# Attention probabilities turned by VectorE squares and a trip through DRAM instead of on TensorE

## The reference

```python
aq, ak, av, bq, bk, bv, cq, ck, cv, cg, gates = jnp.split(h @ w_in[l], split_points, axis=-1)
y_a = diff_attention(qa, ka, va, lam, lam_init, a_subln[l])   # 4 heads: softmax - lam * softmax, width 128
y_b = chunk_attention(qb, kb, vb, b_rel_bias[l])              # 8 heads: softmax with relative bias, width 64
y_c = retention(qc, kc, vc, cg.astype(f32), c_out_norm[l])    # 4 heads: scores * decay, no softmax
```

## Time and profile before

| | |
|---|---|
| median of 3 runs | 1818.6 us (1818.33 to 1820.05) |
| profiled execution, first to last instruction (span) | 1816.7 us |
| time of that execution outside the span | not recorded apart; median less span is 1.9 us |
| PE busy | 1797.5 us, 99% |
| POOL busy | 1365.0 us, 75% |
| DVE busy | 942.8 us, 52% |
| ACT busy | 905.1 us, 50% |
| DMA | 366.61 MB, mean 202 GB/s |
| granted TensorE clock, mean | 0.999 of full speed |

### The profile page before, as it was taken

One profiled execution on the slowest core, in us unless ns is written; L12 is line 12 of the kernel. 1 busy time (PEld: TensorE's weight loads), 2 busy tenths in 40 slices (PEclk: granted clock), 3 DMA queues, 4 the chain that ended last, 5 costly groups with the idle time before them and its releaser, 6 DMA issues.

```text
span 1816.7 us, 25068 instructions
## 1 busy us (share of the span) xinstructions
PE 1797.5 (99%) x9322; PEld 1482.3 (82%) x9322; DVE 942.8 (52%) x1756; ACT 905.1 (50%) x1337; POOL 1365.0 (75%) x568
## 2 busy tenths in 40 slices
PE   6999999999999999999999999999999999999999
PEld 5888888887889888887888888888888878888887
DVE  4673766678655524776553230714095865143152
ACT  3334424764456644455554644464445565545442
POOL 2624544559868898987689798969897858888885
PEclk9999999999999999999999999999999999999999
DMA  9853885748775775565466566567655645656653
GB/s 366 299 201 93 278 301 164 196 157 301 245 279 188 221 216 194 172 209 165 132 187 195 175 195 195 193 184 232 195 195 181 186 139 163 194 160 211 190 194 128
DMA packets 200697, 366.61 MB, mean 202 GB/s; under 512 B 32868, under 2 KB 54356, under 8 KB 200020
## 3 DMA queue, kind: packets, MB, share of 16 engines
q1 hardware_dynamic: 197568, 357.39, 61.6%
q10 hardware_dynamic: 3028, 7.86, 1.1%
HBM read 364.12 MB, written 6.13 MB: 204 GB/s over the span
## 4 chain that ended last, share of the span: by engine, by line
PE 98%; DMA 0%; ACTq 0%; ACT 0%; DVE 0%; POOL 0%; issue 0%; DVEq 0%
PE ps L1258 26%; PE ps L1260 26%; PE ps L1259 26%; PE ps L1384 3%; PE ps L1385 3%; PE ps L1386 3%; PE ps L1949 1%; PE ps L1951 1%; PE ps L1950 1%; PE ps L1306 1%; PE ps L1876 1%; PE ps L1655 1%; PE ps L1626 1%; PE ps L1636 1%; PE ps L1516 1%; PE ps L1921 1%
## 5 line engine op out<-in xcount | busy, mean ns | idle before, releaser
L616 POOL TENSOR_TENSOR w_lo<-raw,w_hi 128x1024 fp32r<-128x1024 f32 x556 | 1346.0, 2458 | 403.4 <-ACT w_hi L654 382.2
L1258 PE MATMUL ps<-w_hi,act_rows_r 128*128 128x512 f32 x2064 | 814.8, 395 | 3.2 <-POOL w_lo L616 3.1
L1260 PE MATMUL ps<-w_hi,act_rows_r 128*128 128x512 f32 x2064 | 804.8, 390 | 0.0
L1259 PE MATMUL ps<-w_lo,act_rows_r 128*128 128x512 f32 x2064 | 804.5, 390 | 0.0
L654 ACT ACTIVATE w_hi<-raw 128x1024 fp32r<-128x1024 f32 x556 | 571.1, 1058 | 359.4 <-DMA raw<-in_ffn_w_up 96.5
L1258 PEld LDWEIGHTS ps<-w_hi,act_rows_r 128*128 128x128 f32 x2064 | 387.9, 188 | 89.9 <-issue 8.6
L1260 PEld LDWEIGHTS ps<-w_hi,act_rows_r 128*128 128x128 f32 x2064 | 387.8, 188 | 81.8
L1259 PEld LDWEIGHTS ps<-w_lo,act_rows_r 128*128 128x128 f32 x2064 | 388.1, 188 | 77.2
L2604 DVE STREAM_TRANSPOSE ps<-proj 32x256 f32<-32x256 f32 (+1 forms) x384 | 166.6, 434 | 6.5
L2585 DVE TENSOR_TENSOR proj<-proj,ps 128x1024 f32<-128x1024 f32 (+1 forms) x18 | 20.4, 1132 | 252.2 <-PE ps L1260 247.8
L1384 PE MATMUL ps<-act_rows_r,w_hi 128*128 128x512 f32 (+1 forms) x288 | 101.4, 352 | 0.0
(11 more groups left out here) (245 smaller groups left out, 1559.9 us busy)
## 6 DMA issues: line engine op xcount, KB each, us to landing
raw<-in_w_in SPq DMA_DIRECT2D x120, 512.0 KB, 3.8
raw<-in_ffn_w_gate SPq DMA_DIRECT2D x88, 512.0 KB, 4.3
raw<-in_ffn_w_up SPq DMA_DIRECT2D x88, 512.0 KB, 4.3
raw<-in_ffn_w_down SPq DMA_DIRECT2D x88, 512.0 KB, 3.4
proj<-in_ada_w SPq DMA_DIRECT2D x39, 512.0 KB, 7.8
pt<-in_ada_w SPq DMA_DIRECT2D x38, 512.0 KB, 6.4
raw<-in_pool_w_in SPq DMA_DIRECT2D x32, 512.0 KB, 7.4
raw<-in_na_w_in SPq DMA_DIRECT2D x32, 512.0 KB, 5.4
```

The lines of the kernel that those rows point to most:

```text
L616: pool.tensor_tensor(w_lo[:, s, :], raw[:, s, :], w_hi[:, s, :].bitcast(F32), ALU.subtract).then_inc(lo_done, 1)
L1258: pe.matmul(o, h, hi, start=start, stop=False)
L1259: pe.matmul(o, h, lo, start=False, stop=False)
L1260: return pe.matmul(o, c, hi, start=False, stop=stop)
```

## The change

The maps of units 0 to 7 are no longer turned on PE. DVE's new `squares_of_map(i)` turns all 32 x 32 squares of a map in one instruction, from `full` to a free part of `proj`. SP's `keep_map` writes the 128 partitions to a DRAM buffer, and after it has landed `place_map` reads them back in four transfers, one per quarter of the partitions, so that square (a, b) comes to the place of (b, a), in `pt`. Both are issued between weight loads: `keep_map(i)` after the load of group 25 + 2i, `place_map(i)` after that of 26 + 2i. PE's `probabilities` and the copies on ACT and DVE go. `values(i)` of units 0 to 3 moves from G = 20 + 2i to 21 + 2i, that of units 4 to 7 from 20 + 2i to 22 + 2i, and both write bank 6; retention stays in bank 7. `combined(i)` moves to G = 22 + 2i and 24 + 2i, `b_high(i)` to 23 + 2i.

```diff
+        def map_blocks(i):
+            return 3 if i < 4 else 6
+        def map_squares(i, dims, at=0, rows=slice(0, P)):
+            return free(proj[rows, 0:1], dims, GATES + 1024 + (i % 2) * 768 + at)
+        def map_turned(i, dims, at=0, rows=slice(0, P)):
+            return free(pt[rows, 0:1], dims, (i % 2) * 768 + at)
+        def mix_out_bank(i):
+            return 6 if i < MIX_SOFT else 7
+        def map_block(i, m):
+            n = map_blocks(i)
+            return map_turned(i, [[n, P]], m) if i < 4 else map_turned(i, [[32 * n, 4], [1, 32]], 32 * m)
+        def map_landed(engine, l, i):
+            engine.wait_ge(maps_in[i % 2], 64 * (MIX_SOFT // 2 * l + i // 2 + 1))
...
+            def keep_map(l, i):
+                sp.wait_ge(dve_done, dve_s.count(("am_t", l, i)))
...
+                n = P * map_blocks(i)
+                sp.dma_start(map_rows[i % 2, :, 0:n], map_squares(i, [[1, n]])).then_inc(maps_kept[i % 2], 16)
+            def place_map(l, i):
+                sp.wait_ge(maps_kept[i % 2], 16 * (MIX_SOFT // 2 * l + i // 2 + 1))
+                if i >= 2:
+                    sp.wait_ge(pe_done, pe_s.count(("ao", l, i - 2)))
+                n = 32 * map_blocks(i)
+                for kq in range(4):
+                    src = bass.AP(map_rows.tensor, i % 2 * P * 768 + n * kq, [[768, 32], [32 * 768, 4], [1, n]])
+                    sp.dma_start(map_turned(i, [[n, 4], [1, n]], 0, slice(32 * kq, 32 * kq + 32)), src).then_inc(maps_in[i % 2], 16)
...
+                        i = (g - MIX_FIRST - SLOTS - 1) // 2
+                        if layer is not None and 0 <= i < MIX_SOFT:
+                            (keep_map if g % 2 else place_map)(layer, i)
...
@@ scalar @@
-                    if G % 2 == 0 and 4 <= (G - MIX_FIRST) // 2 - 2 < MIX_SOFT:
-                        b_high((G - MIX_FIRST) // 2 - 2)
                     i = (G - MIX_FIRST - 1) // 2
                     if G % 2 == 1 and 0 <= i < MIX_SOFT:
-                        if i:
-                            probabilities(i - 1)
                         exponents(i)
+                    if G % 2 == 1 and 4 <= i - 3 < MIX_SOFT:
+                        b_high(i - 3)
...
@@ tensor @@
                     if i < MIX_SOFT:
-                        pe.wait_ge(act_done, act_s.count(("apt0", l, i)))
-                        if i >= 4:
-                            pe.wait_ge(dve_done, dve_s.count(("apt1", l, i)))
+                        map_landed(pe, l, i)
...
-                    read_out(7)
+                    bank = mix_out_bank(i)
+                    read_out(bank)
...
-                    if even and 2 <= i < MIX_UNITS + 2:
+                    if even and 4 <= i - 3 < MIX_SOFT:
+                        values(i - 3)
+                    if even and MIX_SOFT <= i - 2 < MIX_UNITS:
                         values(i - 2)
-                    if not even and 1 <= i <= MIX_SOFT:
-                        probabilities(i - 1)
+                    if not even and 0 <= i - 2 < 4:
+                        values(i - 2)
...
@@ vector @@
+                def squares_of_map(i):
+                    dve.wait_ge(dve_done, dve_s.count(("aj", l, i)))
                     if i >= 2:
+                        dve.wait_ge(maps_kept[i % 2], 16 * (MIX_SOFT // 2 * l + i // 2))
+                    n = map_blocks(i)
+                    dve.transpose(map_squares(i, [[1, n], [32 * n, 4], [n, 32]] if i < 4 else [[32, n], [32 * n, 4], [1, 32]]),
+                                  mix_rows_of(i, [[P, n], [32, 4], [1, 32]])).then_inc(dve_done, dve_s.one(("am_t", l, i)))
...
                         if i < MIX_UNITS:
                             logits(i)
-                        if i >= 2:
+                        if 3 <= i < 7:
+                            combined(i - 3)
+                        if 4 <= i - 4 < MIX_SOFT:
+                            combined(i - 4)
+                        if i >= MIX_SOFT + 2:
                             combined(i - 2)
                         if i < MIX_SOFT:
                             maxima(i)
...
-                    if 5 <= i <= MIX_SOFT:
-                        probabilities(i - 1)
...
                     elif 4 <= i < MIX_SOFT:
                         rows_scaled(i)
+                    if i < MIX_SOFT:
+                        squares_of_map(i)
```

More of the change, by code:

```diff
@@ L169, in program @@
     rel_rows = nc.dram_tensor("rel_rows", (LAYERS, P, REL_PITCH), F32, kind="Internal").ap()
+    map_rows = nc.dram_tensor("map_rows", (2, P, 768), F32, kind="Internal").ap()
     gate_scratch = nc.dram_tensor("gate_scratch", (DEPTH, KC, 2, P), F32, kind="Internal").ap()
@@ L230, in program @@
         decay_in = sem("decay_in")
+        maps_kept, maps_in = ([sem(f"{n}{k}") for k in range(2)] for n in ("maps_kept", "maps_in"))
         out_done = sem("out_done")
@@ L447, in load_bias, with narrow @@
                                       (hp % 2) * 1024 + h * 512 + t * 256), src).then_inc(bias_in[hp % 2], 16)
-            def narrow(w, blocks, nw, stage=None, prev=None, order=None):
+            def keep_map(l, i):
+                sp.wait_ge(dve_done, dve_s.count(("am_t", l, i)))
+                if i >= 2:
+                    sp.wait_ge(maps_in[i % 2], 64 * (MIX_SOFT // 2 * l + i // 2))
+                elif l:
+                    sp.wait_ge(maps_in[i % 2], 64 * (MIX_SOFT // 2 * l))
+                n = P * map_blocks(i)
+                sp.dma_start(map_rows[i % 2, :, 0:n], map_squares(i, [[1, n]])).then_inc(maps_kept[i % 2], 16)
+            def place_map(l, i):
+                sp.wait_ge(maps_kept[i % 2], 16 * (MIX_SOFT // 2 * l + i // 2 + 1))
+                if i >= 2:
+                    sp.wait_ge(pe_done, pe_s.count(("ao", l, i - 2)))
[3 more added lines that the diff above has]
+                    sp.dma_start(map_turned(i, [[n, 4], [1, n]], 0, slice(32 * kq, 32 * kq + 32)), src).then_inc(maps_in[i % 2], 16)
+            def narrow(w, blocks, nw, stage=None, prev=None, order=None, layer=None):
                 v = w.rearrange("(c p) n -> p c n", p=P)
@@ L590, in _ @@
                 ffn_weights(I["ffn1_w_gate_2"][l], I["ffn1_w_up_2"][l], I["ffn1_w_down_2"][l], tables=True)
-                narrow(I["w_in_2"][l], 15, 512, f"mix_in{l}", order=MIX_ORDER)
+                narrow(I["w_in_2"][l], 15, 512, f"mix_in{l}", order=MIX_ORDER, layer=l)
                 for j in range(6):
@@ L1066, in exponents @@
                                            accum_out=stat[:, 16 + k:17 + k]).then_inc(act_done, act_s.one(("ae", l, i, c, t)))
-                def probabilities(i):
-                    act.wait_ge(pe_done, pe_s.count(("at", l, i, 0)))
-                    if i >= 2:
-                        act.wait_ge(pe_done, pe_s.count(("ao", l, i - 2)))
-                    act.activation(pt[:, (i % 2) * 768:(i % 2) * 768 + 384], ps[:, 6, 0:384],
-                                   ACT.Copy).then_inc(act_done, act_s.one(("apt0", l, i)))
                 def y_square(i):
@@ L1096, in b_high @@
                     act.wait_ge(pe_done, pe_s.count(("ao", l, i)))
-                    act.activation(qk_hi[:, MIX_Y[1][2] + i - 4, :], ps[:, 7, 0:SEQ],
+                    act.activation(qk_hi[:, MIX_Y[1][2] + i - 4, :], ps[:, mix_out_bank(i), 0:SEQ],
                                    ACT.Copy).then_inc(act_done, act_s.one(("xhi", f"y1{l}", 0, i - 4)))
@@ L1121, in mix @@
                         evicted(MIX_SILU, ACT.Silu)
-                    if G % 2 == 0 and 4 <= (G - MIX_FIRST) // 2 - 2 < MIX_SOFT:
-                        b_high((G - MIX_FIRST) // 2 - 2)
                     i = (G - MIX_FIRST - 1) // 2
                     if G % 2 == 1 and 0 <= i < MIX_SOFT:
-                        if i:
-                            probabilities(i - 1)
                         exponents(i)
+                    if G % 2 == 1 and 4 <= i - 3 < MIX_SOFT:
+                        b_high(i - 3)
                     if G == 33:
-                        probabilities(MIX_SOFT - 1)
                         act.activation(pj(AV, 512, IN_COLS), pj(AQ, 512, IN_COLS),
@@ L1878, in scores @@
                     held[4] = held[5] = (dve_s, ("al", l, i))
[L1880 to L1888, removed]
                 def values(i):
@@ L1906, in values @@
                                 for c in range(2):
-                                    e = (i % 2) * 768 + c * 384 + (t + kt) * P
-                                    last = pe.matmul(ps[c * HD:(c + 1) * HD, 7, t * P:(t + 1) * P],
-                                                     pj(BV + (2 * (i - 4) + c) * HD, HD, IN_COLS, t=kt), pt[:, e:e + P],
+                                    last = pe.matmul(ps[c * HD:(c + 1) * HD, bank, t * P:(t + 1) * P],
+                                                     pj(BV + (2 * (i - 4) + c) * HD, HD, IN_COLS, t=kt), map_block(i, 3 * c + t + kt),
                                                      start=kt == 0, stop=kt == t)
```

(25 more changed lines are left out.)

## The result

The changed kernel takes 1831.8 us in the median of 4 runs (1831.01 to 1833.43), the kernel before 1818.5 (1818.33 to 1820.05): a ratio of 1.0071, 95% interval 1.0057 to 1.0085, or 13.3 us slower. 1827.4 was forecast, with a range of 1817 to 1835 and 1824 to 1831 for the likeliest case. The profiled execution has a span of 1829.9 us, 13.2 more than before.

The account below looks back on a forecast made before the run. The prediction took PE, 98% of the chain of waits, to bound the kernel. Per layer -3.66 + 3.4 + 4.4 + 0.3 = +4.4, over two layers +8.8 on the median 1818.6, gave 1827.4 us, range 1817 to 1835.

Parts of the forecast that it names:

- transposes gone, breaks closed: 72 map transposes leave PE and groups at G=29 and G=33 run on without a break: 3.66 us less per layer.
- wait at G=31: PE's turn of the last keys waits for logits(7), behind DVE scalings alternating with POOL's subtractions: 4.4 us a layer.
- waits at G=32, 34: PE's values wait for bank 6, read by a combination standing behind logits on DVE: 1.7 twice, 3.4 us a layer.
- maps late: PE waits for maps coming through DRAM: 0.3 us a layer taken, ends 0 and 4.
- step of three in the stationary: Units 0 to 3 read the turned map with a step of three elements: nothing taken, upper bound 2.8 us a layer.
- The trip: Maps' way through DRAM, one write then four reads: 7.9 us at 2.6 landing, against room of 10.0 in unit 0.
- rival (b): Units 0 to 3: the maps' trip through DRAM is late at 4.2 landing, 8 us more, 1835; chance 0.14.
- Rival (a): At G=31 DVE doesn't meet POOL at unit 6: 1817.9, or 1822.4 with a 2.0 us wait; chance 0.28.
- square transposes held like the scalings: On DVE, unit 6 would lose up to one more POOL instruction, 2.4 us, sum 1832; taken as not happening.
- the doubled landing: Units 0 to 3: 384-byte runs might double the reads' landing to 5.2, 1829.5 in all; rows were said to speak against it.

Follow-up runs that it names:

- g1: f2 with `combined(4)` moved on DVE from G=32 to G=31, directly behind `turned`: 1813.4 us, ratio 0.9970 to the kernel before.
- f1: e4 with the stationary of units 0 to 3 read with a step of one element instead of three (other columns multiplied): 1813.4 us, ratio 0.9969.
- e4: The changed kernel with the edits of e1 and e2 together: 1815.6 us, ratio 0.9984 to the kernel before.
- f4: The kernel before with PE turning one block of each three of the maps (24 of 72 transposes): 1815.2 us, ratio 0.9980.
- e1: The changed kernel with DVE combining units 4 and 5 ahead of the logits of units 8 and 9: 1826.4 us, ratio 1.0038.
- e2: The changed kernel with ACT holding its weight splits from G=30 until DVE has scaled the rows of unit 6: 1822.4 us, ratio 1.0020.
- f3: The changed kernel with DVE scaling and turning unit 6 behind the logits and maxima of unit 7: 1835.0 us, ratio 1.0085.
- g3: g1 with maps of units 0 to 3 read by DMA in 128-byte runs, twelve transfers a unit, giving a step of one: 1835.5 us, ratio 1.0094.
- f2: e4 with ACT's `b_high(4)` ahead of its eviction at G=31: 1815.7 us, ratio 0.9983 to the kernel before.

## Why the prediction came out right

The direction, the mechanism and the places were right; the size was 4.5 us short, and 1831.8 lies just above the likeliest case's own range. By its terms, in one layer (layer 0):

| term | forecast | measured |
|---|---|---|
| transposes gone, breaks closed | -3.66 | -3.7 |
| wait at G=31 | +4.4 | +3.8 |
| waits at G=32, 34 | +3.4 | +3.2 |
| maps late | +0.3 | 0 |
| step of three in the stationary | 0 | +1.1 |
| clock at 1.2 GHz after the wait | 0 | +1.5 |
| sum | +4.4 | +5.8 |

The first term and the step have measurements of their own. g1 waits nowhere and keeps full clock in the mix stages; its stage is 2.6 us shorter than before, which is the first term and the step together. The step is 1.1, by f1 against e4; so the first is -3.7. Its parts: 3.2 for 36 transposes at f4's price; 2 x 0.10 for the closed breaks, where two groups that took 2.86 + 0.57 + 2.91 now take 5.67; and about 4 x 0.07 because six products cost less behind a group than behind scores. The 1.5 is 0.80 for the turn and 0.66 for the group behind it. The unrounded terms sum to the 5.8 of the timelines.

*Transposes.* Right in size. *Waits for bank 6.* 1.61 each for the 1.7 taken; e1 removed them by order alone. *Wait at G=31.* The order of events was as worked out from the earlier trace rows: POOL waits for the rotation's addition, the first scaling for POOL, and so on; e2 shows the pair and f3 moves it. It was 0.6 us shorter: the scalings ended 12.4 us after the start of scores(6) (868.50), not 13.05. *The trip.* Landing took 2.8 us for the write and 2.3 for the reads in the median, and an issue 0.43 instead of 0.617; rival (b) did not occur.

*What failed.* Two prices. The prediction took nothing for the step of three elements because "no row has such a load of weights"; its upper end of 2.8 a layer held the 1.1, and the middle would have been the better choice. And the clock: I priced the wait and not what PE does after it. The trace of before had a row for that, at the very wait that the earlier trace rows name. Behind 3.08 us of idleness the long matmuls took 0.63 us instead of 0.39 while the granted clock was 0.50:

```profile
23.75 0.62 PE L1258 MATMUL ps<-w_hi,act_rows_r 128*128 128x512 f32 x1 [3.08 <-POOL w_lo L616]
```
```profile
24.00:27.20 3.20, 3.20 (x9) 0.50 1.06 388
```

A forecast wait of 4.4 us should have carried that price, or at least have widened the range by it. That the total missed by 4.5 us and no more is partly luck: the two missing terms are 2.6 a layer, and the waits and the late maps were taken 1.1 a layer too high. 2 x 1.4 is what the terms leave, which makes 1830.2; the 1.6 us that remain are the 1.2 at the start of the profiled execution, 0.2 more in layer 1 and 0.2 behind it.

Two small sums of the prediction were off, with no effect. Rival (a) without a wait at G=31 gives 1818.1, not 1817.9. By its own slope a square transpose of 384 elements takes 0.59 us, not 0.57; it took 0.71. And 1832, which the prediction gives for square transposes held like the scalings, is near the 1831.8 by accident: none was held, those of 768 elements took 0.98 us each.

## What to carry to other kernels

Where one engine is 98% of the chain, an edit that takes work off it must be read for every buffer that it asks for later: look who reads the buffer, and what stands ahead of that reader in its own program. When an operation is made earlier on one engine, list which shared resource it now meets on another; here exponents that came 1.8 us earlier set POOL's work onto DVE's, and that wait with the slow clock behind it, 5.2 us a layer, cost more than the 3.7 that PE had gained. When a wait is forecast, look in the trace of before for another wait of that length, and at the clock behind it. Three edits of order (e1's, e2's and g1's) turned a loss of 13.3 us into a gain of 5.3.

## What the runs showed of the hardware

- DVE and POOL alternated, one instruction each, where both had scalings and subtractions to do: two pairs met in 5.05 and 5.21 us where the four DVE instructions alone take 1.01. The Trainium skill ("SBUF — State Buffer", Who interferes with whom) gives the shared pair of ports to whichever engine issues first, for its whole instruction. These traces agree: a scaling that began at 875.82, while POOL ran from 875.04 to 877.93, ended at 878.01. The square transposes ran at 0.98 us for 768 elements with POOL idle or busy.
- A load of a stationary 128 x 128 with a step of three elements took 260 ns, with a step of one 192 ns; six products then step 0.90 and 0.58 us.
- The granted clock fell to 0.50 for 3.4 us at a wait of 3.6 us in the changed kernel and at one of 2.0 in e2, and for 10.2 us at one of 6.65 in f3 (6.8 in its layer 1); it stayed at full speed at the waits of 1.08 in e4. The length of the wait alone does not decide: in g3 it stayed at full speed behind waits of 2.90 and 2.76 us and fell behind one of 2.13. The same first wait of 3.09 us at the start came with 6.8 us at 0.50 in the profiles of the changed kernel, e1, e2 and f3, with 3.4 in those of before, e4, f2, g1 and g3, and with none in f1 and f4. What decides it is open.
- Small DMA runs showed no price in the landing of the reads: 48 KB in 384-byte runs landed in 2.0 us, 16 KB in 128-byte runs in 1.8. The issues had one: twelve in a row took SP 5.5 to 6.4 us, four mostly 1.7. So the doubled landing that the prediction weighed for such runs did not show.
